# Low halves of split weights moved by 32 to 128 bytes against the high ones, and six small arrays moved into a raw buffer's tail

## The reference

```python
def swiglu(h, w_gu, w_down):
    u = h @ w_gu
    g, v = u[..., :D_FF], u[..., D_FF:]
    return (jax.nn.silu(g) * v) @ w_down          # D_FF = 2816, D_MODEL = 1024
...
# first_block: x += rglru_mixer(norm(x)); x += swiglu(norm(x))
#              x += nsa_mixer(norm(x));   x += swiglu(norm(x)); x = norm(x)
# second_block: per layer  h += 0.5 * swiglu_2(norm(h))
#                          h += s5_mixer(norm(h))  or  moba_mixer(norm(h))
#                          h += 0.5 * swiglu_2(norm(h))
```

## Time and profile before

| | |
|---|---|
| median of 3 runs | 1679.89 us |
| lowest, highest | 1678.93, 1684.68 us |
| the profiled execution's own time | 1686.76 us |
| its span, first to last instruction | 1685.0 us |
| mean granted TensorE clock | 0.997 |
| TensorE matmuls, weight loads | 1652.6 us (98%), 1608.1 us (95%) |
| DVE, ACT, POOL | 1233.5 us (73%), 831.1 us (49%), 354.0 us (21%) |
| read from memory | 307.39 MB |

### The profile page before, as it was taken

How to read it: one execution, slowest core, us unless ns; L and a number is a source line. 1 busy time by engine, 2 the same in 40 slices (tenths; PEclk the granted TensorE clock), 3 DMA queues, 4 the chain that set the end, 5 groups by cost and what they waited for, 6 DMA issues and landing times.

```text
span 1685.0 us, 34352 instructions
## 1 busy us (share of the span) xinstructions
PE 1652.6 (98%) x14262; PEld 1608.1 (95%) x14262; DVE 1233.5 (73%) x1581; ACT 831.1 (49%) x1104; POOL 354.0 (21%) x425
## 2 busy tenths in 40 slices
PE   7999999999999999999999999999999999999999
PEld 6799999998789999999999999999999999999999
DVE  7897888784868987788755967766676656667663
ACT  5875444453565444354545245454454445555442
POOL 0222012535505123520012212001100027430000
PEclk9999999999999999999999999999999999999999
DMA  8246668775205778555646425565465645336561
GB/s 333 101 145 208 208 219 277 234 276 194 85 2 192 260 255 302 182 174 193 234 167 254 159 100 205 197 223 201 138 213 199 225 160 163 126 129 222 190 239 45
DMA packets 50719, 321.14 MB, mean 191 GB/s; under 512 B 7697, under 2 KB 8913, under 8 KB 20145
## 3 DMA queue, kind: packets, MB, share of 16 engines
q1 hardware_dynamic: 36432, 280.61, 47.5%
q0 software_dynamic: 12736, 36.87, 6.8%
q10 hardware_dynamic: 1440, 2.10, 0.4%
HBM read 307.39 MB, written 10.09 MB: 188 GB/s over the span
## 4 chain that ended last, share of the span: by engine, by line
PE 84%; DVE 9%; DMA 2%; ACT 2%; issue 2%; POOL 1%; DVEq 0%; ACTq 0%; POOLq 0%
PE bank L2254 25%; PE bank L2255 24%; PE bank L2256 24%; DVE w_lo L1437 3%; PE bank L2536 1%; PE bank L2903 1%; ACT w_hi L1007 1%; PE bank L2855 1%; PE bank L2721 1%; DMA b_raw<-in_s_b 1%; PE bank L2546 1%; PE bank L2610 1%; PE bank L2441 1%; DVE rstd L1447 1%; DVE xc L1688 1%
## 5 line engine op out<-in xcount | busy, mean ns | idle before, releaser
L1437 DVE TENSOR_TENSOR w_lo<-raw,w_hi 128x1024 fp32r<-128x1024 f32 (+2 forms) x486 | 652.6, 1346 | 272.4 <-ACT w_hi L1007 271.5
L1007 ACT ACTIVATE w_hi<-raw 128x1024 fp32r<-128x1024 f32 (+2 forms) x486 | 538.0, 1117 | 537.5 <-PE bank L2256 506.7
L2254 PE MATMUL bank<-hg_hi,w_hi 128*128 128x256 f32 x2648 | 741.1, 280 | 14.5 <-DVE hg_lo L1442 10.3
L2255 PE MATMUL bank<-hg_lo,w_hi 128*128 128x256 f32 x2648 | 736.5, 278 | 0.0
L2256 PE MATMUL bank<-hg_hi,w_lo 128*128 128x256 f32 x2648 | 736.4, 278 | 0.0
L2254 PEld LDWEIGHTS bank<-hg_hi,w_hi 128*128 128x128 f32 x2648 | 499.6, 189 | 19.6 <-DVE w_lo L1437 12.2
L2256 PEld LDWEIGHTS bank<-hg_hi,w_lo 128*128 128x128 f32 x2648 | 499.9, 189 | 0.0
L2255 PEld LDWEIGHTS bank<-hg_lo,w_hi 128*128 128x128 f32 x2648 | 497.9, 188 | 0.2
L2254 PE MATMUL bank<-hid,w_hi 128*128 128x256 f32 x1056 | 294.9, 279 | 1.1 <-DVE h L1474 1.1
L2255 PE MATMUL bank<-hid,w_hi 128*128 128x256 f32 x1056 | 294.2, 279 | 0.0
L2256 PE MATMUL bank<-hid,w_lo 128*128 128x256 f32 x1056 | 294.2, 279 | 0.0
(11 more groups left out here) (414 smaller groups left out, 2038.4 us busy)
## 6 DMA issues: line engine op xcount, KB each, us to landing
raw<-in_w SPq DMA_DIRECT2D x189, 1024.0 KB, 4.9
raw<-in_w SPq DMA_DIRECT2D x48, 1408.0 KB, 6.3
raw<-in_w SPq DMA_DIRECT2D x8, 768.0 KB, 5.0
b_rows<-in_s_b_rows POOLq DMA_DIRECT2D x8, 512.0 KB, 8.1
l_rows<-s_powers POOLq DMA_DIRECT2D x64, 64.0 KB, 10.4
s_ca<-cp_s POOLq DMA_DIRECT2D x8, 512.0 KB, 4.6
s_ba<-ba_s POOLq DMA_DIRECT2D x8, 512.0 KB, 7.4
ba_slot<-s_ba POOLq DMA_DIRECT2D x8, 512.0 KB, 4.9
```

The lines of the kernel that those rows point to most:

```text
L1007: act.activation(w_hi[s][:, 0:n], raw[r][:, c * n:(c + 1) * n], ACT.Copy).then_inc(hi_made, 1)
L1437: dve.tensor_tensor(w_lo[s][:, 0:n], raw[r][:, c * n:(c + 1) * n], w_hi[s][:, 0:n].bitcast(F32), ALU.subtract).then_inc(lo_made, 1)
L2254: pe.matmul(psum, w_hi_ap, x_hi_ap, start=first, stop=False, **kw)
L2255: pe.matmul(psum, w_hi_ap, x_lo_ap, start=False, stop=False, **kw)
```

## The change

`w_lo[s]` is placed 32, 64, 96 or 128 bytes (for s = 0 to 3) further behind `w_hi[s]`, and `place[0]` is rounded up so that every `w_hi` stays where it was modulo 128 bytes. The arrays `tiny` and `tiny_i` get no place of their own any more: they are columns of `raw[0]`, 768 floats ahead of its end. The gap ahead of the phases' region is computed, so that the region starts at the place of hg modulo 128. No instruction is added or removed.

```diff
         place[0] += 32
+        w_at = place[0]
         w_hi, w_lo = [], []
         for s in range(SPLIT):
             w_hi.append(sb(f"w_hi{s}", [P, UNIT_MAX // 2], F32R))
+            place[0] += 32 * (s + 1)
             w_lo.append(sb(f"w_lo{s}", [P, UNIT_MAX // 2], F32R))
+            place[0] += (w_at - place[0]) % 128
         vec = sb("vec", [P, NVEC])
...
         sp4 = sb("sp4", [P, RT])
-        tiny = [sb(f"tiny{i}", [P, 32]) for i in range(5)]
-        tiny_i = sb("tiny_i", [P, 32], I32)
+        tiny = [raw[0][:, UNIT_MAX - 768 + 32 * i:UNIT_MAX - 768 + 32 * i + 32] for i in range(5)]
+        tiny_i = raw[0][:, UNIT_MAX - 768 + 160:UNIT_MAX - 768 + 192].bitcast(I32)
...
-        place[0] += 96
+        place[0] += (hg_at - place[0]) % 128
         region = (place[0], nc.sbuf_usable_end // 32 * 32)
```

## The result

The changed kernel takes 1716.16 us in the median (1715.36 to 1717.06, 4 runs) against 1679.41 for the kernel before (1673.84 to 1684.68, 4 runs): 2.2% slower, ratio 1.0219, interval 1.0186 to 1.0253. The interval lies clear of 1. The prediction was 1688, with a range up to 1704. The direction of its likeliest case, slower with a chance of 0.44, was right and the size was not: the loss is 36.7 us where 8.1 were forecast.

What follows compares the result with a forecast made beforehand. The prediction took TensorE's locked-in pace to bound the kernel. The profiled 1686.8 us plus 9.4 for the moved low loads gave 1696.2; against the median, 6.9 below the profiled execution, 1689, taken as 1688 us, range 1664 to 1704.

Steps and rivals of the forecast that it cites:

- likeliest case: Three-pass lines: low loads at new residues disturb the rhythm, mildly or fully; slower, 1685 to 1708 us, chance 0.42 (slower overall 0.44).
- TensorE's pace, and not a wait, sets the time: Whole kernel: matmuls follow at 113.3 or about 118 ns; three-pass lines wait only some 15 us in all.
- The splits and the small arrays: DVE's subtraction and ACT's copy stay hidden behind matmuls, and tiny arrays in raw0's tail cost nothing; both terms nothing.
- the nearest row for a load at another residue: Three-pass lines: each of 3042 moved low loads costs 3.1 ns more, 9.4 us in all.
- The waits left as they were: Whole kernel: no instruction, transfer or semaphore added or removed, no queue changed, so no term for waits.
- The upper bound of 28.3 us: Three-pass lines, slots 0 to 2: one odd load spoils its whole triple, 9126 gaps at 3.1 ns.
- rival in which the whole triple is spoilt: Slots 0 to 2: all three gaps at 118 ns, about 1708 us; chance 0.42 shared with the mild form.
- Subtracting 6.9 us: Whole kernel: the median of the runs, 1679.9, lies 6.9 us below the profiled 1686.8, so the sum was lowered.
- The kick out of the slow rhythm: Three-pass lines: odd low loads end the slow pace, leaving all triples at 113.3 ns; 1667 us, chance 0.33.
- Weight loads don't care: Three-pass lines: only the moving operand's place counts, so paces are merely redrawn; 1680 us, some 6 either side, chance 0.25.

Runs made afterwards that it cites:

- e1: The changed kernel with all four low weights 128 bytes further behind the high ones in place of four different offsets: 1667.67 us, 0.9952 of the kernel before.
- e2: The changed kernel with all four low weights 32 bytes further behind the high ones: 1728.05 us, 1.0307 of the kernel before.
- e4: The changed kernel with all four low weights 96 bytes further behind the high ones: 1710.13 us, 1.0202 of the kernel before.
- e8: e1 with high and low weights both 64 bytes further, at the moving operands' residue modulo 128: 1719.88 us, 1.0236 of the kernel before.
- e11: e1 with 32 more bytes ahead of the gate weights, so that rec lies at 0 modulo 128 as hg does: 1667.20 us, 0.9886 of the kernel before.
- e5: The changed kernel without any offset of the low weights, only small arrays and region moved: 1675.14 us, 0.9979 of the kernel before.
- e9: e1 with the low weights of slot 2 alone at 96 bytes, as in the changed kernel: 1691.16 us, 1.0065 of the kernel before.
- e6: The changed kernel without offset of the low weights but with slots 128 bytes further apart: 1670.18 us, 0.9942 of the kernel before.
- e10: The changed kernel with the four high arrays together, then the four low ones, 128 bytes further: 1666.66 us, 0.9893 of the kernel before.
- e3: The changed kernel with all four low weights 64 bytes further behind the high ones: 1712.29 us, 1.022 of the kernel before.
- e15: The changed kernel with low arrays together at 192 modulo 256, as in e10, and rec at 0 modulo 128: 1665.33 us, 0.9901 of the kernel before.

## Why the prediction was wrong in size

- *That TensorE's pace, and not a wait, sets the time, and that an address can change it.* Right, and shown: e1 against e2 to e4 and e8 for the loads, e11 for the moving operand.
- *The splits and the small arrays at nothing.* Right: 1340 and 1116 ns, and e5 is level with the kernel before.
- *"I take the nearest row for a load at another residue, 118 ns against the mean of 114.9: 3.1 ns".* This step failed, in the number of gaps that it was multiplied by. One odd load does not lengthen one gap by 3.1 ns: its triple grows by 9 to 11 ns over the 344.5 of before (table), near what the sentence on the upper bound had, and slot 3, counted as unchanged, grows by 12. The halves of 2.83 to 2.85 us are 118.3 ns over all four slots. Reckoned in the prediction's own way, the term should have been 12,168 gaps x (118.3 - 114.9) = 41 us, where it had 9.4.
- *The waits left as they were.* That was off the other way. Between the profiled executions TensorE's busy time grew by 38.4 us and its idle time fell by 8.9, so the execution went from 1686.8 to 1716.3 us, by 29.6 and not by 41.
- *The upper bound of 28.3 us* left out slot 3, a quarter of all triples, because it took a rhythm to be a property of the addresses. My own rows spoke against that: the earlier trace rows show two paces at one set of addresses. A state that lasts can also be handed on, which e9 shows. The range was narrower still: it ended at 1704, below the 1708 of its own rival in which the whole triple is spoilt, the one that came nearest.
- *Subtracting 6.9 us to get from the profiled execution to the median.* The sum was 1696 before this. That correction stands for slow stretches that a typical run before has fewer of; but the changed kernel has no fast stretches in the windows above to win, and its runs lie within 1.7 us, with the profiled one (1716.33) close to the median. The correction belonged to the kernel before alone, and it is why the medians lie 36.7 us apart and the profiled executions 29.6.
- *The kick out of the slow rhythm.* As a forecast for this change it was wrong: no low load at 96, 0 or 32 leaves the fast pace to its own slot. Something like it is there with another step: e6 and e10 break the symmetry by 128 bytes, keep the residue modulo 128, and show no slow pace in either window; the stretch with rec stays slow in both.
- *"Weight loads don't care".* This rival is out: e2 differs from e1 in the place of the low weights alone and takes 60 us more. The Trainium skill says in "TensorE: Matmul & The Clock Gate", Step-by-step: what each phase is for, that a load takes no SBUF read bandwidth from the running matmul. The trace does not agree with the rule as strictly read: in the last half of the changed kernel, with every other engine and the DMA queues idle, the pace is 118.8 ns, and the place of the loads decides whether it is that or 113.4 as in e1. Whether the rule fails or the delay arises somewhere else than at the read ports, no run tells; why 64 bytes between loads and moving operand is the good distance, and why e2's even and odd slots differ, stays open, and so does token_major, for which no placement was tried that held the fast pace throughout.

## What to carry to other kernels

Where TensorE alternates loads and matmuls without a gap, look at the distance from start to start, by stretch, before anything else. In this kernel two values for the same work meant a rhythm that lasts, and then the byte distance between stationary and moving operands was a setting worth some per cent: try the distances modulo 128 bytes, then break the symmetry among the loads by 128. Price such a change for all of the stream and not for the instructions that it touches. A wide scatter of repeated runs hints at two paces; a narrow one of four runs proves little.

## What the runs showed of the hardware

- With 256 columns moving and 128 x 128 loads of float32r, a matmul costs 113.3 ns or 117.7 ns at the same clock and addresses, for stretches of over 170 us.
- Low loads moved by 32 bytes cost 3.6% against 128 bytes (1728.05 to 1667.67 us), with the same instructions and data.
- The fast pace was seen only where the loads lie 64 bytes modulo 128 from the moving operand (113.3 ns in e1, 119.7 in e2 and 117.9 in e3). With hg and hid, where some loads lie 128 apart modulo 256, the windows show no slow stretch (e6, e10); with rec that was not enough (118.8 ns in e15). The same shift of all operands by 32 bytes changes nothing (1665.45 against 1666.66 us).
- The slow pace needs no other engine and no DMA at work: 118.8 ns in the last half of the changed kernel, 113.4 in that of e1 (32 gaps, 1655.14 to 1658.77 us).
- At one set of residues modulo 128 a half takes 2.92 or 2.83 us in e2, by its slot's place modulo 256.
- A slot at one set of addresses takes 2.72 or 2.85 us, as the slot ahead of it leaves the stream.
- e10 beats the kernel before by 1.1% (0.9832 to 0.9955, 4 runs) and needs no other change than places.
